# GpSimd takes half of the probability scaling, transposes go in half tiles, and the expert stage reorders its gather

## The reference

```
# first block: each of 16 experts takes its 64 best tokens
aff = softmax(h @ w_router)
top_aff, top_idx = top_k(aff.T, 64)
xs = h[top_idx]
a = silu(xs @ w_gate_e) * (xs @ w_up_e)
y = (a @ w_down_e) * top_aff[..., None]
out = zeros.at[top_idx].add(y)

# second block, per layer, 8 heads of 64, query blocks of 128
p = exp(s - max(s)) / sum(exp(s - max(s)))      # window, compressed, selected, window, latent
o = (gate *) p @ v
```

## Time and profile before

| | us |
|---|---|
| median of 3 runs | 3249.96 |
| lowest and highest | 3247.2, 3250.67 |
| the profiled execution | 3246.58 |
| its span | 3244.8 |
| granted clock of PE, mean share | 0.996 |
| PE busy, DVE busy in the span | 3143.7, 1519.7 |
| ACT busy, POOL busy in the span | 683.7, 246.1 |
| section 0 of the first layer, about | 1075 to 1122 |
| section 1 of the first layer, about | 1248 to 1337 |

### The profile page before, as it was taken

One profiled execution on the slowest core, in us unless ns is written; L12 is line 12 of the kernel. 1 busy time (PEld: TensorE's weight loads), 2 busy tenths in 40 slices (PEclk: granted clock), 3 DMA queues, 4 the chain that ended last, 5 costly groups with the idle time before them and its releaser, 6 DMA issues.

```text
span 3244.8 us, 38028 instructions
## 1 busy us (share of the span) xinstructions
PE 3143.7 (97%) x14982; PEld 2140.0 (66%) x14982; DVE 1519.7 (47%) x2982; ACT 683.7 (21%) x1409; POOL 246.1 (8%) x179
## 2 busy tenths in 40 slices
PE   7999999999999999999999999999989999999998
PEld 2445874444433586775865888857768578578887
DVE  2254663221113747736634554446585465255433
ACT  2042220000003416414021000023371231300000
POOL 3400010000000113010011000000201001100000
PEclk9999999999999999999999999999999999999999
DMA  7341248999996121120222222321202212122221
GB/s 295 107 162 43 82 166 317 409 405 387 406 409 240 45 86 53 40 85 33 83 80 76 80 91 86 102 68 65 98 8 78 72 40 101 61 73 91 91 85 71
DMA packets 120144, 435.70 MB, mean 134 GB/s; under 512 B 13216, under 2 KB 15008, under 8 KB 119200
## 3 DMA queue, kind: packets, MB, share of 16 engines
q1 hardware_dynamic: 114768, 417.91, 34.7%
q10 hardware_dynamic: 5200, 15.37, 1.2%
HBM read 429.03 MB, written 4.19 MB: 134 GB/s over the span
## 4 chain that ended last, share of the span: by engine, by line
PE 84%; issue 6%; DVE 5%; ACT 1%; DMA 1%; DVEq 1%; POOL 1%; POOLq 1%; ACTq 0%; SPq 0%
PE bank L713 82%; PE bank L1410 2%; DMA ring<-in_stream 1%; DVE arena L2781 1%; DVE arena L2751 1%; DVE arena L2753 1%; DVE arena L2778 0%; DVEq L2749 0%; DVE bank L2732 0%; POOLq L2062 0%; POOLq L2065 0%; DVE bank L2742 0%; POOL arena L2063 0%; ACT arena L1794 0%; DVE arena L2331 0%
## 5 line engine op out<-in xcount | busy, mean ns | idle before, releaser
L713 PE MATMUL bank<-arena 128*128 128x256 f32 (+10 forms) x5760 | 980.4, 373 | 31.9 <-issue 9.7
L713 PEld LDWEIGHTS bank<-arena 128*128 128x128 f32 (+4 forms) x5760 | 666.2, 172 | 305.3 <-issue 191.7
L713 PE MATMUL bank<-arena,ring 128*128 128x256 f32 (+2 forms) x1952 | 515.3, 418 | 4.4 <-DVE y L2216 1.8
L713 PE MATMUL bank<-h,ring 128*128 128x256 f32 (+2 forms) x1776 | 512.6, 445 | 1.6 <-issue 1.3
L713 PEld LDWEIGHTS bank<-arena,ring 128*128 128x128 f32 (+1 forms) x1952 | 345.3, 185 | 154.4 <-issue 106.2
L713 PEld LDWEIGHTS bank<-h,ring 128*128 128x128 f32 (+1 forms) x1776 | 326.1, 188 | 148.1 <-issue 111.7
L2073 POOL TENSOR_TENSOR sq<-sq 128x512 f32<-128x512 f32 (+1 forms) x67 | 88.1, 1315 | 2320.9 <-ACT sq L1621 2320.9
L713 PE MATMUL bank<-ring,arena 128*64 128x512 f32 (+2 forms) x976 | 227.1, 603 | 18.8 <-ACT arena L1640 11.7
L713 PE MATMUL bank<-y,arena 128*128 128x256 f32 (+1 forms) x1064 | 239.0, 381 | 0.0
L713 PE MATMUL bank<-y,ring 128*128 128x256 f32 (+1 forms) x800 | 227.1, 439 | 0.0
L713 PEld LDWEIGHTS bank<-y,arena 128*128 128x128 f32 x1064 | 202.1, 190 | 29.2 <-issue 1.9
(11 more groups left out here) (335 smaller groups left out, 2794.0 us busy)
## 6 DMA issues: line engine op xcount, KB each, us to landing
ring<-in_stream SPq DMA_DIRECT2D x581, 512.0 KB, 4.5
arena<-in_stream SPq DMA_DIRECT2D x132, 512.0 KB, 12.3
h<-in_stream SPq DMA_DIRECT2D x42, 512.0 KB, 11.8
sig<-in_stream SPq DMA_DIRECT2D x21, 512.0 KB, 11.4
sq<-in_stream SPq DMA_DIRECT2D x21, 512.0 KB, 11.8
x<-in_xT ACTq DMA_DIRECT2D x1, 2048.0 KB, 11.2
arena<-memory_kv ACTq DMA_DIRECT2D x4, 512.0 KB, 6.7
outT<-h ACTq DMA_DIRECT2D x8, 256.0 KB, 2.1
```

What stands on the lines that cost most here:

```text
L713: ins = pe.matmul(out, lhsT, rhs, start=start, stop=stop, skip_group_check=loose)
```

## The change

Four things are changed together.

1. In the experts, `gather(pair + 1)` is cut in halves; the second follows the transposes of the activations, on PE and in ScalarE's copies.
2. `choose` is made in another way: GpSimd multiplies `selx` by the affinities for each pair (`shares`), PE turns the four blocks, VectorE copies them. The constants `cidx` and `pairsel` and the tile `affT` go.
3. In sections 0 to 2 a transpose of 128 query rows is made as two of 64 rows, into two banks; the value products read their operand from both.
4. In all units of section 0, and in section 1 in those from the seventh on that aren't compressed ones, GpSimd scales side 1 and VectorE side 0 alone. PE waits for side 1 between the sides. The first layer's scaling of x on GpSimd moves ahead to the time after section 0. Some semaphores are merged so that there are enough.

```diff
-CSE, N_CSE = columns([("iota", CAP), ("cidx", 1), ("pairsel", 8 * P)])
+CSE, N_CSE = columns([("iota", CAP)])
...
+                u["shared"] = sec == 0 or sec == 1 and s >= 6 and u["kind"] != "cmp"
...
-            def gather(pair):
-                if pair:
-                    pe.wait_ge(silu_made, 2 * pair)
-                for half in range(2):
+            def gather(pair, halves=(0, 1)):
+                for half in halves:
+                    if pair:
+                        pe.wait_ge(silu_made, 2 * pair - 1 + half)
...
             def choose(pair):
                 if pair:
                     pe.wait_ge(spread_taken, 8 * pair)
-                for i, src in enumerate((slot, affT)):
-                    mm(bank[:, 4 + i, :], cse[0:E, so + P * pair:so + P * pair + P], src, True, True
-                       ).then_inc(selw_in, 1)
+                pe.wait_ge(shared, pair + 1)
+                for m in range(TT):
+                    ins = pe.transpose(bank[:, 4, P * m:P * m + P], shares[pair % 2][:, P * m:P * m + P], c_("ident"))
+                ins.then_inc(selw_in, 1)
...
                 if pair < E // 2 - 1:
-                    gather(pair + 1)
+                    gather(pair + 1, (0,))
...
                     ins.then_inc(a_turned, 1)
+                if pair < E // 2 - 1:
+                    gather(pair + 1, (1,))
...
                             for side in range(2):
+                                if side == 1 and u["shared"]:
+                                    pe.wait_ge(side_scaled, l * len(SHARED) + SHARED_AT[u["n"]] + 1)
                                 for b in range(u["nb"]):
-                                    ins = pe.transpose(bank[:, 4 + side, P * b:P * b + P],
-                                                       probs[:, n % 3, side, P * b:P * b + P], c_("ident"))
+                                    if sec == 3:
+                                        ins = pe.transpose(bank[:, 4 + side, P * b:P * b + P],
+                                                           probs[:, n % 3, side, P * b:P * b + P], c_("ident"))
+                                        continue
+                                    at = 64 * (u["nb"] * side + b)
+                                    for i, r in enumerate((slice(0, 64), slice(64, P))):
+                                        ins = pe.transpose(bank[:, 4 + i, at:at + 64],
+                                                           probs[r, n % 3, side, P * b:P * b + P], c_("ident")[r, r])
...
-                                ins = mm(bank[part, 6 + og % 2, cols], v, probsT[:, n % 2, side, block_],
-                                         start, stop, loose=True)
+                                at = 64 * (u["nb"] * side + block_.start // P)
+                                ins = mm(bank[part, 6 + og % 2, cols], v, probsT[:, n % 2, side, block_] if sec == 3
+                                         else probsT[:, n % 2, :, at:at + 64], start, stop, loose=True)
...
+            def scale_side(l, u):
+
+                n = l * N_UNITS + u["n"]
+                pool.wait_ge(stat_made, RECIPROCAL_AT[l, u["n"]])
+                for j in range(u["subs"]):
+                    p = probs[:, n % 3, 1, u["nk"] * j:u["nk"] * (j + 1)]
+                    r = rden[:, n % 4, u["subs"] + j:u["subs"] + j + 1]
+                    if u["gate"] is None:
+                        ins = pool.tensor_scalar(p, p, r, None, ALU.mult)
+                    else:
+                        g = u["gate"][j][1]
+                        ins = pool.tensor_scalar(p, p, r, sgate[:, u["qt"], g:g + 1], ALU.mult, ALU.mult)
+                ins.then_inc(side_scaled, 1)
+
             def tile_sums_made(l):
 
+                for u in SECTION[0]:
+                    scale_side(l, u)
+                if l == 0:
+                    first_scaling()
                 for name, _, _ in SEVEN:
                     if name == "lat0":
                         for j in range(2):
                             late_turn(l, j)
+                        for u in SECTION[1]:
+                            if u["shared"]:
+                                scale_side(l, u)
...
+                if key == "rms_2":
+                    pool.wait_ge(sel_ready, TT)
+                    for pair in range(E // 2):
+                        if pair >= 2:
+                            pool.wait_ge(selw_in, pair - 1)
+                        pool.tensor_tensor(shares[pair % 2].rearrange("p (m e c) -> p m e c", m=TT, e=2),
+                                           selx[:, :, 2 * pair:2 * pair + 2, :],
+                                           aff[:, 2, :, 2 * pair:2 * pair + 2].rearrange("p m (e c) -> p m e c", c=1)
+                                           .to_broadcast([P, TT, 2, CAP]), ALU.mult).then_inc(shared, 1)
...
-            dve.tensor_copy(work, N.bank(n1("affT"))[0:E, :])
-            take(N, n1("affT"), affT, m=E)
+            take(N, n1("affT"), work, m=E)
...
             def choose(pair):
-                dve.wait_ge(selw_in, 2 * pair + 2)
-                dve.tensor_scalar(tmp[:, :], bank[:, 4, :], ce_("cidx"), None, ALU.is_equal)
-                dr()
-                dve.tensor_tensor(selw[:, pair % 2, :], tmp[:, :], bank[:, 5, :], ALU.mult).then_inc(selw_made, 1)
+                dve.wait_ge(selw_in, pair + 1)
+                dve.tensor_copy(selw[:, pair % 2, :], bank[:, 4, :]).then_inc(selw_made, 1)
...
-                                for i in range(2 * u["subs"]):
+                                for i in range(u["subs"] if u["shared"] else 2 * u["subs"]):
```

More of the change, by code:

```diff
@@ L342, in two_blocks @@
         cse = carve(N_CSE)
+        shares = [carve(T) for _ in range(2)]
+        top8 = carve(8)[0:E, :]
         h2k = carve(4096, "p (m n) -> p m n", m=TT)
@@ L354, in two_blocks @@
         selw = carve(2 * T, "p (b t) -> p b t", b=2)
-        rows = carve(4 * T, "p (a t) -> p a t", a=4)
-        affT, work, slot, mark = [rows[0:E, i, :] for i in range(4)]
+        rows = carve(3 * T, "p (a t) -> p a t", a=3)
+        work, slot, mark = [rows[0:E, i, :] for i in range(3)]
         aff = carve(3 * TT * E, "p (a m e) -> p a m e", a=3, m=TT)
@@ L497, in two_blocks @@
         sel_ready, xs_made, xs_taken = sem("sel_ready"), sem("xs_made"), sem("xs_taken")
[L498 removed]
+        shared, selw_in, selw_made = sem("shared"), sem("selw_in"), sem("selw_made")
         spread_made, spread_taken = sem("spread_made"), sem("spread_taken")
@@ L635, in two_blocks, with reciprocals @@
         SECTION = [[u for u in UNITS if u["sec"] == s] for s in range(4)]
+        for sec, us in enumerate(SECTION):
+            for s, u in enumerate(us):
+                u["shared"] = sec == 0 or sec == 1 and s >= 6 and u["kind"] != "cmp"
+        SHARED = [u["n"] for u in UNITS if u["shared"]]
+        SHARED_AT = {n: i for i, n in enumerate(SHARED)}
+        def reciprocals():
+            at, told = {}, 0
+            for l in range(LAYERS):
+                for us in SECTION:
+                    for s in range(len(us) + 1):
+                        if s < len(us) and us[s]["kind"] == "cmp":
+                            told += 1
+                        if s >= 1:
+                            told += 3 if us[s - 1]["kind"] == "cmp" else 1
+                            at[l, us[s - 1]["n"]] = told
+            return at
+        RECIPROCAL_AT = reciprocals()
         kv_d = [nc.dram_tensor(f"memory_kv{l}", (P, 2048), F32, kind="Internal").ap() for l in range(LAYERS)]
@@ L1756, in sines, with take_xs @@
                 act.activation(s_, s_, ACT.Sin).then_inc(sin_made, 1)
-            def take_xs(pair):
-                for half in range(2):
+            def take_xs(pair, halves=(0, 1)):
+                for half in halves:
                     act.wait_ge(xs_made, 2 * pair + half + 1)
@@ L1790, in _ @@
                 if pair < E // 2 - 1:
-                    take_xs(pair + 1)
+                    take_xs(pair + 1, (0,))
                 for half in range(2):
@@ L1795, in _ @@
                                    bank[:, 4 + half, :], ACT.Copy).then_inc(aT_ready, 1)
+                if pair < E // 2 - 1:
+                    take_xs(pair + 1, (1,))
                 if pair < 2:
@@ L2038, in late_turn, with first_scaling @@
                 pool.tensor_tensor(Q[:, 6 + j, :], Q[:, 6 + j, :], rot[:, at % 2, :], ALU.add).then_inc(pool_made, 1)
+            def first_scaling():
+                pool.wait_ge(rstd_made, NORMS["rms_f1"][0] + 3)
+                for k in range(KD):
+                    pool.tensor_scalar(x[:, k, :], x[:, k, :], gfirst[:, k:k + 1], None, ALU.mult)
+                    pool.drain()
+                    pool.tensor_tensor(x[:, k, :], x[:, k, :], rstd[:, 1, :], ALU.mult).then_inc(x_made, 1)
+            def scale_side(l, u):
[10 more added lines that the diff above has]
+                ins.then_inc(side_scaled, 1)
             def tile_sums_made(l):
+                for u in SECTION[0]:
```

(5 more changed lines are left out.)

36 lines of the change are left out of this document (11 added, 25 removed).

## The result

| | before | after |
|---|---|---|
| median, us | 3250.32 (4 runs) | 3228.10 (4 runs) |
| lowest and highest | 3247.2, 3250.96 | 3225.3, 3229.06 |
| the profiled execution | 3246.58 | 3225.3 |
| mean granted clock of PE in it | 0.996 | 0.993 |

The ratio is 0.9934, 95% interval 0.9922 to 0.9946: the change makes the kernel 21.5 us faster (17.5 to 25.4). The prediction was 8.3 us, 3242, with a range down to 3230.

The account below looks back on a forecast made before the run. PE was taken to bound the kernel, with DMA in the experts and VectorE in attention. Experts -9.5, half transposes -2, GpSimd's side +4, x scaling -0.8 sum to -8.3: 3242 us against the median 3250.0, range 3230 to 3254.

Parts of the forecast that it names:

- cut by the weights: Experts: 15.7 us of PE time saved, but weight loading at 409 GB/s limits the gain to 9.5 us (6 to 10.8).
- So a pair costs what a whole one costs: Sections 0 to 2: two 64-row transposes take as long as one 128x128; only a shape change goes, 2 us in all.
- rival E: Half transposes overlap in full: 0.055 less per block, 9 us in section 2, some 6 elsewhere, 3227 us; chance 0.03.
- The loop: Section 0: the cycle binding a unit to the one two later, 4.43 us with GpSimd scaling the second head.
- I take the product's fixed part, 0.36, and the rest in proportion: GpSimd's scaling time by width, from 1.64 us at 512: 1.0 at 256, 1.3 at 384, 0.7 at 128.
- the bounds (0.31 to 1.64): GpSimd's scaling at 256 wide, in us: a copy's time in proportion below, no saving from 512 wide above.
- +1.6 a layer: Section 1: GpSimd's share lengthens units, +0.8 for 384 wide, +0.5 for joined 2x256, +0.3 for the other widths.
- rival B: GpSimd is quick on narrow tiles, up to 0.8 us at 256: attention -5 to -12, 3232 us; chance 0.22.
- 16 us without cover: Shared units: GpSimd's simultaneous start stretches VectorE's scaling, 0.4 us in some 20 units a layer if slack hides none.
- x scaling: Section 1, first layer: moving GpSimd's scaling of x out removes contention with VectorE, -0.8 us.

Follow-up runs that it names:

- triple repeat: The changed kernel, with PE repeating side 0's transposes three times in section 0 while it waits for side 1; 3221.84 us, ratio 0.9919 (0.9905 to 0.9932).

## Why the prediction was wrong

**Experts, right.** -9.5 forecast with a cut by the weights. The start of section 0 moved by 8.2 in the change and 7.2 in the run of these edits, whose timed gain is 5.2 (2.3 to 8.1). The 409 GB/s, the new waits for landings and the missing waits for ScalarE are as stated, and that the two edits don't add up is shown by taking them apart. Only the waits for weights are fewer, 3.8 us for about 6. The last product of the experts ends at 1004.7 where it ended at 1012.9 before; forecast was near 1002.

**Half transposes, the step that failed most.** "So a pair costs what a whole one costs" compared eight whole transposes with eight pairs of loads for the scores, both near 1.02 us. But those score records move 128 columns through each half of the array and a half transpose moves 64, since its identity is 64 wide. The rows did show the pair at work: two matmuls of 128 columns in the time of one whole. For 64 columns that means half. Measured: 0.048 us less a block, near rival E's 0.055. The term was -2 (bounds 0 and 13); section 2, priced at nothing, gives 3.0 us a layer, section 1 some 2 to 4, and the timed run -6.8 even with a worse clock. That the prediction put 0.03 on E rests on this one reading of a row.

By the Trainium skill, "TensorEngine Tiling (Array Packing)", Theoretical Speedup, a dimension of 64 or less gives up to 2x; the trace agrees here, 0.11 to about 0.06 us a block.

**GpSimd's share, model right and a price wrong.** The loop came to 4.44 us for 4.43 forecast. With whole transposes in section 0 and so without falls, the sharing leaves it 0.4 and 0.5 us longer than before, for +0.3 to +0.5 forecast; with halves it costs about nothing there. What failed is "I take the product's fixed part, 0.36, and the rest in proportion" for all widths and both forms, from a row of the one-scalar form. For that form it was good (1.08). The two-scalar form takes 0.64 at 256 and 0.87 at 384, inside the bounds (0.31 to 1.64) but far from the value. Section 1, forecast at +1.6 a layer, gives -2.4. So rival B (quick GpSimd) held in section 1 and the forecast in section 0, for a reason that neither had: the form. The contention that the prediction priced at nothing, with 16 us without cover, is small indeed: VectorE's scalings 256 wide take 353 ns in the mean for 352 without a gate, and with one, in the joined units, 497 for 410.

The Trainium skill, "GPSIMD Engine Reference", Engine selection, keeps elementwise work on VectorE but calls one-input work on GpSimd roughly line rate. The trace bears out the first and not the second: VectorE's scalings 256 wide take 0.35 us (0.41 with a gate), GpSimd's 1.08 (0.64 with one). In section 1 the sharing pays all the same, 2.4 us a layer; the two engines work at the same time there.

**The clock, not foreseen.** The text had no term for TensorE's granted clock, though the profile before shows it falling elsewhere. After the change PE does the same work in less time between the same waits, and the clock falls in section 0. That costs some 9 us in the profiled execution (about 4 in the first layer, 5 in the second; an estimate from its units and the pause behind them, against the same ones in runs without a fall there). That half transposes bring it on is shown by four runs: half transposes alone have 0.992, the change without GpSimd 0.992, whole transposes 0.996, whole ones in section 0 alone 0.996. The profiles say the same: the seven executions with whole transposes in section 0 (the kernel before and six of the runs) have no fall in that section; the six with halves and no triple repeat each have one at least. That it is PE's shorter work and not the shape of the tiles is what the repeats speak for: they keep the shape and lengthen the work. That GpSimd's waits add to it isn't settled: without them in section 0 the clock is at 0.994, with shorter ones too.

**x scaling, right**, 1.1 for 0.8, and too small to be timed.

Summed, roughly and from the profiles: experts -8; half transposes -15 (3.0 a layer in section 2, up to 3.8 in section 1, 1 to 2 in section 0) with the clock left out; GpSimd's share and x in section 1 some -6 to -7; the clock +7 to +10. That is about the -21.3 between the two executions.

## What to carry over

Before you hold two rows of the matrix engine against each other, compare the columns that move through, not only rows and count: a transpose cut into two, each with half the rows and half the moving columns, costs half of the whole here (0.06 us for 0.11). Price an operation on GpSimd by a row of its own form, since one scalar more can be quicker. And where a change shortens PE's work between waits that stay, add a term for the clock: read its column stretch by stretch in both kernels.

## What the runs showed of the hardware

- On GpSimd a TENSOR_SCALAR with one multiplication takes 1083 ns at 256 columns and 698 at 128; with a second one, by a scalar from memory or by 1.0, 640 and 467 to 484. At 512 it is 1.64 us (one) against 1.03 (two).
- A 128x128 transpose as two of 64 rows takes 0.048 us less, by the spacing of the units in section 2 (3.36 us for 3.75 with eight blocks), and the two halves start together, 3 to 4 ns apart.
- With transposes that only repeat earlier ones the granted clock stayed at 2.4 GHz in section 0 of the profiled execution, and the kernel came out some 5 us faster.
- The mean clock tracks the time from run to run: of 21 runs of the kernel before those at 0.996 took 3244.6 to 3248.2 us, those at 0.993 or 0.994 took 3250.1 to 3250.8.
